# A hybrid attention and delta-rule block: the conditioning projection in four column groups, and four projection units in the prologue

## The chip, the cores and the metric

The kernel runs on one core of a Trainium2 chip. The metric is the time of one execution on the device in microseconds (us): 898.84, the median of 3 runs (898.61 to 899.08).

## What is computed

x is 512 rows of 1024. A vector c of 1024 gives shift and scale (and a gate, used at the end) by a product with w_ada; the normalised x is scaled and shifted and becomes h. h is projected by w_in onto many blocks of columns, which feed a sparse attention branch and a gated delta-rule branch. Both are merged by gates, projected by w_o and added to x.

```python
mod = c @ w_ada + b_ada                      # (1, 3072)
shift, scale, gate = jnp.split(mod, 3, axis=-1)
h = rmsnorm(x, pre_norm_gain) * (1.0 + scale[:, None, :]) + shift[:, None, :]
proj = h @ w_in                              # (512, 10840)
# attention branch: partial_rope on q, k and on the indexer's q_idx, k_idx
# (angles = positions * inv_freq), indexer scores, top 128 keys, softmax
# delta branch: conv of width 4 and silu on q, k, v; per chunk a triangular
# inverse, then a scan over the chunks
y = jax.nn.sigmoid(ga) * y_a + jax.nn.sigmoid(gb) * y_b
return x + gate[:, None, :] * rmsnorm(y @ w_o, post_norm_gain)
```

## The kernel before

All data are float32. Work is kept transposed: 128 channels on the partitions, 512 positions along the free dimension. One projection of h onto 128 columns is a **unit**. Weights are split into a high part (fp32r, made by ScalarE, L926) and a low part (made by GpSimd, L1216), h likewise, and a unit is 8 k tiles times 3 matmuls of 512 columns (L588 to L590), accumulated in one PSUM bank. The list UNITS (L57) gives the order: S (a small unit with the indexer's key and the decay columns), the keys K0 to K5, the indexer's queries I0 to I3, gates GA0 to GA3, then for each head Q, V, Z and one more, then the attention's units, and the merge. The weights of a unit go through a ring of four buffers, its result through three PSUM banks; the unit that takes a bank waits until the one three before it has been read (take_wait, L417).

The order of the work is written out by hand in **rounds**: each round r has a quarter of a unit on TensorE (two k tiles, six matmuls, `part`, L600), and every engine's program has a loop over r in which each step stands in a round of its own. R_KEY, R_LOW, R_GRAM, R_INV, R_DELTA, R_ATT and others (L79 to L87) say in which round the steps of a head begin: the taps of the key's convolution on VectorE (L1552), the decay tiles, the Gram matrix and its norms, the inversion of 16x16 blocks for four heads at a time (`invert`, L1599, 30 dependent small steps, then through DRAM into the tiles U and T), the solve and scan of the delta rule. In a round TensorE does the scan, solve, attention, Gram, small and logit matmuls first and its quarter unit last (L870 to L884).

Ahead of the rounds is the prologue. SyncE issues all loads in one queue: the small rows, constants, x (2 MB), positions, two small vectors, eight tiles of w_ada (1 MB each, whole rows), then weights. VectorE makes four rotary tables' arguments for two frequency sets side by side, 128x1024 (L1364 to L1391); ScalarE takes their sines (L937 to L939). TensorE computes c @ w_ada as matmuls with c broadcast to 128 columns (the tile cb) as the stationary operand and 512 columns of w_ada moving, in four banks (`condition`, L625): 32 fp32 matmuls, 64 instructions, half ahead of the transposes of x and half behind. Each row of the result is the same vector, so VectorE takes the diagonal of sixteen 128x128 blocks by a multiply with the identity and a reduction (L1404) to have it on the partitions. Then h is made per k tile: scale and shift on VectorE (L1416), high part on ScalarE (L948), low part on VectorE (L1420), and TensorE does the units S and K0 k by k behind it (L646 to L650). Round 0 starts with unit 2 (K1).

Of the kernel before, what the change touches and what calls it, by code (L numbers as in the profile page):

```python
# [15 lines left out]
P = 128  # L16
# [29 lines left out]
(C_ID, C_TRIU, C_TRIL, C_FILL, C_ONES, C_M16, C_M32, C_MLOW, C_MUP) = range(9)  # L46
N_CST = 9
SUB = 16

# [7 lines left out]
UNITS = ([("S", 0), ("K", 0)] + [("K", h) for h in range(1, 6)] + [("I", n) for n in range(4)]  # L57
# [10 lines left out]
N_ROUNDS = 4 * (Q_OUT - 2)  # L68


def begins(kind, h):
    return 4 * (UNITS.index((kind, h)) - 2)
# [12 lines left out]
R_ATT = [192] + [188 + 16 * h for h in range(1, HEADS)]  # L85
# [6 lines left out]
def constants():  # L92
# [50 lines left out]
def program(nc, ctx, x, c, positions, w_ada, b_ada, pre_gain, post_gain, w_in, ln_gain, ln_bias, conv_w, a_log,  # L143
# [19 lines left out]
    cols = place("cols", [P, 4 + SUB * SUB])  # L163
# [108 lines left out]
    def bank(b):  # L272
        return ps[:, b, :]
# [48 lines left out]
    def steps(name, names):  # L322
        return Steps(sem(name), names)

    s_rows, s_cst, s_pos, s_x, s_sc, s_bc, s_xres, s_out = (sem(n) for n in (
        "rows_loaded", "constants_loaded", "positions_loaded", "x_loaded", "scalars_loaded", "gate_rows_loaded",
        "residual_loaded", "output_stored"))
    s_ada = [sem(f"w_ada_loaded{k}") for k in range(KT)]
# [11 lines left out]
    pro_pe = steps("pro_pe", ["rowsT", "rows2T"] + [f"x{k}" for k in range(KT)] + ["mod"])  # L340
    pro_act = steps("pro_act", [f"ssq{i}" for i in range(NT)] + ["sinA", "sinI", "cos"] + [f"x{k}" for k in range(1, KT, 2)]
                    + [f"hi{k}" for k in range(KT)])
    pro_dve = steps("pro_dve", ["pcol", "pcol2", "cb", "hgain", "posf", "angA", "angI", "turns", "whole", "r1", "r2", "r3", "rc",
                                "wrap", "rc2", "clamp", "clampc"]
                    + [f"xn{i}" for i in range(NT)] + [f"x{k}" for k in range(0, KT, 2)]
                    + [f"m{b}" for b in range(16)] + ["mb", "scg", "h0"]
                    + [f"{a}{k - (a == 'lo')}" for k in range(1, KT) for a in ("h", "lo")] + [f"lo{KT - 1}"])
# [73 lines left out]

    def unit_bank(kind, h):
        return UNITS.index((kind, h)) % PROJ_BANKS
# [8 lines left out]
    def _(sp):  # L432
        sp.dma_start(prow[R_CONV:R_CONV + 96, :], conv_w.rearrange("w (m p) -> (w m) p", p=P)).then_inc(s_rows, 16)
# [3 lines left out]
        for r, v in ((R2_LNG, ln_gain), (R2_LNB, ln_bias)):  # L437
            for n in range(2):
                sp.dma_start(prow2[r:r + 1, n * IDX_DIM:(n + 1) * IDX_DIM],
                             v.rearrange("(a n) -> a n", a=1)).then_inc(s_rows, 16)  # L440
        sp.dma_start(prow2[R2_NG:R2_NG + 1, :], norm_gain.rearrange("(a n) -> a n", a=1)).then_inc(s_rows, 16)
        sp.dma_start(cst[:], cst_in).then_inc(s_cst, 16)
        sp.dma_start(cols[:], cols_in).then_inc(s_cst, 16)
        sp.dma_start(x_sb[:], x.rearrange("(i p) d -> p i d", p=P)).then_inc(s_x, 16)
        sp.dma_start(pos_i[:], positions.to_broadcast([P, S])).then_inc(s_pos, 16)
        sp.dma_start(small_cols[:, 48:56], a_log.rearrange("(a n) -> a n", a=1).to_broadcast([P, 8])).then_inc(s_sc, 16)
        sp.dma_start(small_cols[:, 56:64], dt_bias.rearrange("(a n) -> a n", a=1).to_broadcast([P, 8])).then_inc(s_sc, 16)
        for k in range(KT):
            sp.dma_start(w_ada_sb[:, k, :], w_ada[k * P:(k + 1) * P, 0:2 * D]).then_inc(s_ada[k], 16)
# [5 lines left out]
        wv = w_in.rearrange("(k p) n -> p k n", p=P)  # L455
        n_ik = IDX_DIM + IDX_HEADS
        sp.dma_start(raw[:, 0, :, 0:n_ik], wv[:, :, COL_IK:COL_IK + n_ik]).then_inc(s_raw[0], 16)
        sp.dma_start(raw[:, 0, :, n_ik:N_SMALL], wv[:, :, COL_BETA:COL_BETA + 2 * HEADS]).then_inc(s_raw[0], 16)
# [80 lines left out]
        for q in range(1, RING):  # L539
            load(q)  # L540
        for r in range(-13, N_ROUNDS + 8):
            if (r - 3) % 4 == 0 and RING <= (r - 3) // 4 + 8 < len(UNITS):
                load((r - 3) // 4 + 8)
# [35 lines left out]
    def _(pe):  # L579

        def project(q, rhs_hi, rhs_lo, ks, m=P):

            slot, out_ap = q % RING, ps[0:m, q % PROJ_BANKS, :]
# [16 lines left out]
        def part(r):  # L600

            q, quarter = r // 4 + 2, r % 4
            kind = UNITS[q][0]
            if quarter == 0 and q >= PROJ_BANKS:
                take_wait(pe, q - PROJ_BANKS)
# [13 lines left out]
        EARLY = 4  # L619
        pe.wait_ge(s_rows, 16 * 9)  # L620
        pe.wait_ge(s_cst, 32)
        pe.transpose(ps[:, 2, 0:P], prow[:], ident).then_inc(*pro_pe.inc("rowsT"))
        pe.transpose(ps[:, 2, P:P + 3], prow2[:], ident[0:3, 0:3]).then_inc(*pro_pe.inc("rows2T"))

        def condition(ks):  # L625
            for k in ks:
                pe.wait_ge(s_ada[k], 16)
                for n in range(4):
                    mm = pe.matmul(bank(2 + n), cb[:, k, :], w_ada_sb[:, k, n * S:(n + 1) * S], start=(k == 0),  # L629
                                   stop=(k == KT - 1))  # L630
            return mm

        pe.wait_ge(*pro_dve.at("cb"))
        pe.wait_ge(*pro_dve.at("pcol2"))
        condition(range(EARLY))
        XB = [0, 1, 6, 7]
        for k in range(KT):
            if k == 0:
                pe.wait_ge(*pro_dve.at(f"xn{NT - 1}"))
            if k >= 4:  # L640
                pe.wait_ge(*(pro_dve if k % 2 == 0 else pro_act).at(f"x{k - 4}"))
            for i in range(NT):
                mm = pe.transpose(ps[:, XB[k % 4], blk(i)], x_sb[:, i, blk(k)], ident)
            mm.then_inc(*pro_pe.inc(f"x{k}"))
        condition(range(EARLY, KT)).then_inc(*pro_pe.inc("mod"))
        for k in range(KT):  # L646
# [26 lines left out]
        def logits(r):  # L673

            for m, (hd, qt) in enumerate(LOGITS):
                if r != ends_at("I", hd // 2) + 4 + m % 6 // 2:
                    continue
# [1165 lines left out]
```

## Time and profile before

| | |
|---|---|
| median of 3 runs | 898.84 us |
| profiled execution | 899.64 us |
| its span | 897.8 us |
| mean granted TensorE clock | 0.983 of full |
| ScalarE busy | 326.7 us, 36% |
| GpSimd busy | 392.6 us, 44% |

The span runs from the first to the last instruction that the profiler recorded on the core; some 1.8 us of the profiled execution lie around it. Busy time is the time in which an engine has at least one instruction running. Matmuls overlap each other, so a matmul's own duration is longer than the distance from its start to that of the next, and a busy TensorE is not a TensorE at its peak. TensorE's granted clock is given as a share of full speed.

### The profile page before, as it was taken

The page shows a single profiled execution, that of the slowest core. Times are in us where ns is not written, and L with a number is a line of the kernel's source. Part 1 is how long each engine was busy: PE and PEld are TensorE (multiplying, and loading weights), DVE is VectorE, ACT ScalarE, POOL GpSimd, SP SyncE. Part 2 cuts the span into 40 slices and gives each one's busy share as a digit, 9 for nine tenths or more (in the row PEclk, how much of TensorE's full clock was granted, in tenths as well). Part 3 has the DMA queues.
Part 4 walks back from the last instruction along what each step waited for, and adds up shares of the span by engine and source line. Part 5 has one row for each costly group of instructions (what it writes and reads, how often), then busy time and mean ns, then how long its engine had stood idle before and what let it go on. Part 6 is the DMA issues. An engine that isn't in the chain of part 4 may idle for free.

```text
span 897.8 us, 11319 instructions
## 1 busy us (share of the span) xinstructions
PE 832.9 (93%) x4226; PEld 672.3 (75%) x4226; DVE 473.0 (53%) x907; ACT 326.7 (36%) x678; POOL 392.6 (44%) x262
## 2 busy tenths in 40 slices
PE   1978688999999989999999999999999999999996
PEld 0546565688888778888888777777777788878996
DVE  3455889826668777665666544445434433232104
ACT  2424432444352434425434344443334322212211
POOL 1123554355264434644535544354543543543542
PEclk9989889999999999999999999999999999999998
DMA  7933530533232332323221222232222245452502
GB/s 273 334 88 124 171 92 8 120 103 110 63 104 61 106 81 61 93 61 106 83 70 48 71 70 71 71 92 72 71 71 71 74 142 160 141 171 86 194 19 94
DMA packets 147345, 92.10 MB, mean 103 GB/s; under 512 B 17746, under 2 KB 140883, under 8 KB 146011
## 3 DMA queue, kind: packets, MB, share of 16 engines
q1 hardware_dynamic: 147290, 91.38, 34.9%
q8 instruction: 34, 0.56, 0.3%
q14 instruction: 21, 0.16, 0.1%
HBM read 84.52 MB, written 6.85 MB: 102 GB/s over the span
## 4 chain that ended last, share of the span: by engine, by line
PE 71%; DVE 18%; ACT 4%; issue 3%; DMA 2%; POOL 1%; SPq 0%; POOLq 0%; ACTq 0%; DVEq 0%
PE ps L588 15%; PE ps L590 15%; PE ps L589 15%; PE ps L629 3%; DVE yq L1552 2%; PE ps L859 2%; PE ps L907 2%; PE ps L906 2%; PE ps L905 2%; PE ps L846 2%; DVE binv L1611 2%; ACT prob L1144 2%; DVE kraw L1552 1%; DMA pos_i<-in_positions 1%; DVE prob L1721 1%
## 5 line engine op out<-in xcount | busy, mean ns | idle before, releaser
L1216 POOL TENSOR_TENSOR w_lo<-raw,w_hi 128x1024 fp32r<-128x1024 f32 (+1 forms) x109 | 263.5, 2423 | 351.5 <-ACT w_hi L926 351.4
L588 PE MATMUL ps<-h_hi,w_hi 128*128 128x512 f32 (+1 forms) x680 | 291.0, 428 | 6.0 <-ACT h_hi L948 6.0
L590 PE MATMUL ps<-h_hi,w_lo 128*128 128x512 f32 (+1 forms) x680 | 269.1, 396 | 0.0
L589 PE MATMUL ps<-h_lo,w_hi 128*128 128x512 f32 (+1 forms) x680 | 267.7, 394 | 0.0
L588 PEld LDWEIGHTS ps<-h_hi,w_hi 128*128 128x128 f32 (+1 forms) x680 | 129.8, 191 | 32.5 <-ACT h_hi L948 6.8
L590 PEld LDWEIGHTS ps<-h_hi,w_lo 128*128 128x128 f32 (+1 forms) x680 | 128.8, 189 | 29.8 <-issue 0.5
L589 PEld LDWEIGHTS ps<-h_lo,w_hi 128*128 128x128 f32 (+1 forms) x680 | 129.7, 191 | 26.1 <-issue 3.6
L926 ACT ACTIVATE w_hi<-raw 128x1024 fp32r<-128x1024 f32 (+1 forms) x109 | 113.3, 1050 | 18.2 <-PE ps L907 17.1
L1085 ACT ACTIVATE o_tok<-ps 128x128 f32<-128x128 f32 x32 | 8.9, 278 | 107.4 <-PE ps L811 107.2
L629 PE MATMUL ps<-w_ada_sb,cb 128*128 128x512 f32 x64 | 30.2, 633 | 11.5 <-DVE rp L1376 11.5
L906 PE MATMUL ps<-w_lo,y_hi 128*128 128x256 f32 x128 | 36.2, 283 | 0.0
L907 PE MATMUL ps<-w_hi,y_lo 128*128 128x256 f32 x128 | 36.2, 283 | 0.0
L905 PE MATMUL ps<-w_hi,y_hi 128*128 128x256 f32 x128 | 36.2, 283 | 0.0
L1726 DVE SCALAR_TENSOR_TENSOR oat<-ps,za 128x512 f32<-128x512 f32 x8 | 5.5, 692 | 55.7 <-PE ps L859 55.7
L629 PEld LDWEIGHTS ps<-w_ada_sb,cb 128*128 128x128 f32 x64 | 12.9, 205 | 27.3 <-issue 15.7
L1738 DVE SCALAR_TENSOR_TENSOR ysum<-th_b,ps 128x512 f32<-128x512 f32 x8 | 5.5, 686 | 51.4 <-PE ps L590 51.4
L1694 DVE TENSOR_TENSOR qk<-qk,sw 32x1024 f32<-32x1024 f32 x8 | 24.6, 3074 | 13.8 <-POOL qk L1313 13.8
L1172 ACT ACTIVATE y_hi<-ysum 128x512 fp32r<-128x512 f32 x8 | 5.1, 633 | 73.5 <-DVE ysum L1749 73.5
L1144 ACT ACTIVATE prob<-prob,amx 128x128 f32<-128x128 f32 (+3 forms) x32 | 17.6, 552 | 30.6 <-DVE amx L1714 30.6
L1313 POOL TENSOR_TENSOR qk<-qk,tab_cos 32x1024 f32<-32x1024 f32 x8 | 27.1, 3382 | 1.1 <-DVE sw L1687 1.1
L1545 DVE MAX8 m<-score 128x8 f32<-128x256 f32 (+2 forms) x48 | 26.5, 551 | 0.0
L1547 DVE MATCH_REPLACE8 score<-m,score 128x256 f32<-128x256 f32 (+2 forms) x48 | 26.1, 543 | 0.0
(274 smaller groups left out, 1445.8 us busy)
## 6 DMA issues: line engine op xcount, KB each, us to landing
raw<-in_w_in SPq DMA_DIRECT2D x84, 512.0 KB, 3.8
w_ada_sb<-in_w_ada SPq DMA_DIRECT2D x8, 1024.0 KB, 19.5
raw<-in_w_b_out SPq DMA_DIRECT2D x8, 512.0 KB, 3.8
raw<-in_w_a_out SPq DMA_DIRECT2D x8, 512.0 KB, 4.1
ada<-in_w_ada SPq DMA_DIRECT2D x8, 512.0 KB, 4.8
raw<-in_w_o SPq DMA_DIRECT2D x8, 512.0 KB, 4.0
inverse_tiles<-zero SPq DMA_DIRECT2D x2, 1032.0 KB, 5.0
x_sb<-in_x SPq DMA_DIRECT2D x1, 2048.0 KB, 10.0
```

The source lines that it names most:

```text
L588: pe.matmul(out_ap, w_hi[:, slot, k, 0:m], rhs_hi(k), start=(k == 0), stop=False)
L589: pe.matmul(out_ap, w_hi[:, slot, k, 0:m], rhs_lo(k), start=False, stop=False)
L590: mm = pe.matmul(out_ap, w_lo[:, slot, k, 0:m], rhs_hi(k), start=False, stop=(k == KT - 1))
L629: mm = pe.matmul(bank(2 + n), cb[:, k, :], w_ada_sb[:, k, n * S:(n + 1) * S], start=(k == 0), stop=(k == KT - 1))
L905: pe.matmul(o_ap, y_hi[k][:, blk(t)], w_hi[:, pair, k, :], start=(k == 0), stop=False)
L906: pe.matmul(o_ap, y_hi[k][:, blk(t)], w_lo[:, pair, k, :], start=False, stop=False)
L907: mm = pe.matmul(o_ap, y_lo[k][:, blk(t)], w_hi[:, pair, k, :], start=False, stop=(k == KT - 1))
L926: act.activation(w_hi[:, slot, :, 0:n], raw[:, slot, :, 0:n], ACT.Copy).then_inc(hi_made, 1)
L1144: act.activation(prob[:, keys(qt)], prob[:, keys(qt)], ACT.Exp, bias=amx[:, 1, qt:qt + 1], scale=HD ** -0.5, accum_out=amx[:, 2, qt:qt + 1 ...
L1216: pool.tensor_tensor(w_lo[:, slot, :, 0:n], raw[:, slot, :, 0:n], w_hi[:, slot, :, 0:n].bitcast(F32), ALU.subtract).then_inc(lo_made, 1)
L1313: pool.tensor_tensor(qk2[h % 2][0:32, :, :], qk2[h % 2][0:32, :, :], tab_cos[0:32, 0:1, :].to_broadcast([32, 2, S]), ALU.mult).then_inc(*r ...
L1552: dve.scalar_tensor_tensor(out=y[:, n:S], in0=src[:, 0:S - n], scalar=pcol_at(R_CONV + (3 - n) * 24 + j * 8, h), in1=y[:, n:S], op0=ALU.mu ...
```

## The change

- **w_ada in four column groups.** Group g holds 256 columns of the shift and the same 256 of the scale, all eight k tiles: two loads of 1 MB in rows of 1 KB. VectorE multiplies the k tiles 0 to 5 by c (one per partition) and adds them up (`mod_sum`); TensorE reduces over the partitions with 12 fp32 matmuls that have one moving column: for each of four 128-column blocks the k tiles 6 and 7 against c, and `mod_sum` against ones. The result is on the partitions at once; the sixteen diagonal reductions and the tile cb go. Three small VectorE ops per group then give shift and scaled gain.
- **h per group.** ScalarE makes h (Identity with scale and bias) and its high part for two k tiles per group, and VectorE the low part. All copies of the transposed x are on ScalarE, four banks in turn.
- **Four units in the prologue.** S, K0, K1 and K2 accumulate k by k as h arrives, in four banks (S in bank 7): S and K0 with k 0 to 3, then K1 and K2 with k 0 to 3, then all four with k 4 to 7. Round 0 starts with unit 4 (K3), and there are eight rounds fewer.
- **Rotary tables.** Both frequency sets share one 128x512 argument: partitions 32 to 63 carry the main one. Four sines; the main tables are made on partitions 32 to 63 of `tab_a` and moved to partitions 0 to 31 by two loads.
- **Queues.** x goes in four tiles on ScalarE's queue, with the small rows behind it; positions and the first constants lead SyncE's queue.
- **Rounds.** In TensorE's loop `part(r)` stands first. The key, decay, Gram, inversion and logit steps have new rounds; where the new number is the old one less eight, nothing moves against the units.

```diff
-UNITS = ([("S", 0), ("K", 0)] + [("K", h) for h in range(1, 6)] + [("I", n) for n in range(4)]
+FIRST_UNITS = 4
+UNITS = ([("S", 0)] + [("K", h) for h in range(6)] + [("I", n) for n in range(4)]
...
-N_ROUNDS = 4 * (Q_OUT - 2)
+N_ROUNDS = 4 * (Q_OUT - FIRST_UNITS)
...
-R_KEY = [ends_at("K", h) for h in range(HEADS)]
-R_LOW = [10, 11, 13, 14, 17, 18, 46, 50]
-R_GRAM = [13, 15, 17, 19, 22, 26, 74, 90]
-R_INV = [25, 97]
+R_KEY = [0, 2, 4, 6, 9, 12, ends_at("K", 6), ends_at("K", 7)]
+R_LOW = [8, 9, 10, 11, 13, 14, 38, 42]
+R_GRAM = [10, 13, 16, 19, 22, 25, ends_at("K", 6) + 5, ends_at("K", 7) + 5]
+R_INV = [27, R_GRAM[7] + 6]
+R_LOGIT = [ends_at("I", m // 6) + 6 + m // 6 + m % 6 // 2 for m in range(24)]
...
+        conditioning(0)
+        load_small()
+        load(1)
+        conditioning(1)
+        load(2)
+        load(3)
+        conditioning(2)
+        conditioning(3)
+        sp.dma_start(cst[:, 2:, :], cst_in[:, 2:, :]).then_inc(s_cst, 16)
+        sp.wait_ge(*pro_act.at("cosA"))
+        sp.dma_start(tab_sin[0:32, 0, :], tab_a[32:64, 0, :]).then_inc(s_tab, 16)
+        sp.dma_start(tab_cos[0:32, 0, :], tab_a[32:64, 1, :]).then_inc(s_tab, 16)
...
+        def conditioning(g):
+
+            pe.wait_ge(s_ada[g], 32)
+            pe.wait_ge(*pro_dve.at(f"a{g}_{DIRECT[0] - 1}"))
+            if g < 2:
+                pe.wait_ge(*pro_act.at(f"x{KT - 4 + g}"))
+            else:
+                pe.wait_ge(*pro_dve.at(f"g{g - 2}"))
+            for n in range(2):
+                for t in range(2):
+                    out_ap = ps[:, 3 + g % 2, 2 * n + t:2 * n + t + 1]
+                    for k in DIRECT:
+                        pe.matmul(out_ap, w_ada_sb[:, g, n, k, blk(t)], pcol[:, 0, R_C + k:R_C + k + 1], start=(k == DIRECT[0]),
+                                  stop=False)
+                    mm = pe.matmul(out_ap, mod_sum[:, g, n, blk(t)], ones[:, 0:1], start=False, stop=True)
+            mm.then_inc(*pro_pe.inc(f"mod{g}"))
...
+        conditioning(0)
+        conditioning(1)
+        first_rows((0, 1), (0, 1))
+        conditioning(2)
+        first_rows((0, 1), (2, 3))
+        first_rows((2, 3), (0, 1, 2, 3))
+        conditioning(3)
+        first_rows((0, 1, 2, 3), (4, 5, 6, 7))
...
         for r in range(N_ROUNDS):
+            part(r)
             for h in range(HEADS):
                 scan(h, r - R_DELTA[h])
...
-            part(r)
...
+        def conditioned(g):
+
+            act.wait_ge(*pro_dve.at(f"g{g}"))
+            for k in (2 * g, 2 * g + 1):
+                act.wait_ge(*pro_act.at(f"x{k}"))
+                act.activation(xT[:, k, :], xT[:, k, :], ACT.Identity, scale=small_cols[:, 24 + k:25 + k],
+                               bias=small_cols[:, 8 + k:9 + k]).then_inc(*pro_act.inc(f"h{k}"))
+                act.wait_ge(*pro_act.at(f"h{k}"))
+                act.activation(h_hi[:, k, :], xT[:, k, :], ACT.Copy).then_inc(*pro_act.inc(f"hi{k}"))
...
+        for g in range(GROUPS):
+            conditioning(g)
+            if g > 0:
+                low_rows(2 * g - 2)
+                low_rows(2 * g - 1)
+            modulation(g)
+        low_rows(KT - 2)
+        low_rows(KT - 1)
```

## Rows read from the trace of the kernel before

**Rows 1.** The page, part 1: busy us, share of the span, instructions.
```profile
PE 832.9 (93%) x4226; PEld 672.3 (75%) x4226; DVE 473.0 (53%) x907; ACT 326.7 (36%) x678; POOL 392.6 (44%) x262
```

**Rows 2.** Stretches, all engines: length, busy us (instructions), granted clock, DMA share, GB/s.
```profile
0.00:60.00 60.00, 34.49 (x99) 17.16 (x100) 22.64 (x64) 16.73 (x23) 11.55 (x12) 0.99 0.76 260
60.00:62.00 2.00, 2.00 (x6) 1.40 (x5) 2.00 (x5) 1.26 (x2) 0.00 (x0) 0.50 0.00 0
73.40:185.90 112.50, 93.24 (x388) 71.05 (x387) 96.57 (x184) 46.16 (x90) 53.70 (x41) 0.92 0.37 96
185.90:195.50 9.60, 9.60 (x44) 7.96 (x43) 0.03 (x1) 3.30 (x7) 4.66 (x3) 1.00 0.54 146
195.50:897.80 702.30, 682.22 (x3654) 566.63 (x3652) 347.11 (x648) 256.36 (x553) 319.85 (x204) 1.00 0.31 90
```

**Rows 3.** Timeline of the prologue: start, duration, engine, line, operation [idle before, releaser].
```profile
14.69 1.06 ACT L932 ACTIVATE xT<-x_sb 128x1024 f32<-128x1024 f32 x1 [12.69 <-DMA x_sb<-in_x]
20.27 2.00 POOL L1228 TENSOR_TENSOR small_cols<-small_cols,nhalf 128x4 f32<-128x4 f32 x1
26.49 2.73 DVE L1395 TENSOR_SCALAR x_sb<-x_sb,small_cols 128x1024 f32<-128x1024 f32 x4
36.27 3.66 PE L643 MATMUL ps<-cst,x_sb 128*128 128x128 f32 x32
53.70 0.29 DVE L1404 CUSTOM_DVE_ANT_0 scratch<-ps,cst 128x128 f32<-128x128 f32 x1 [13.48 <-PE ps L629]
59.65 0.70 PE L588 MATMUL ps<-h_hi,w_hi 128*88 128x512 f32 x1 [5.98 <-ACT h_hi L948]
```

**Rows 4.** Timeline, TensorE: cold matmuls, two Gram groups, last matmuls of units 13 and 14.
```profile
61.43 0.63 PE L589 MATMUL ps<-h_lo,w_hi 128*128 128x512 f32 x1
61.85 0.63 PE L590 MATMUL ps<-h_hi,w_lo 128*128 128x512 f32 x1
...
97.86 1.05 PE L698 MATMUL ps<-kraw 128*128 128x128 f32 x8
...
109.53 2.05 PE L698 MATMUL ps<-kraw 128*128 128x128 f32 x8 [7.88 <-DVE L L1595]
...
189.95 0.39 PE L590 MATMUL ps<-h_hi,w_lo 128*128 128x512 f32 x1
...
195.39 0.39 PE L590 MATMUL ps<-h_hi,w_lo 128*128 128x512 f32 x1
```

**Rows 5.** Timeline of VectorE and GpSimd: first tap, one swish twice, last score fill.
```profile
74.42 2.32 DVE L1552 SCALAR_TENSOR_TENSOR kraw<-ps,pcol,kraw 128x511 f32<-128x511 f32 x3 [7.72 <-ACT kraw L999]
...
100.73 2.77 POOL L1216 TENSOR_TENSOR w_lo<-raw,w_hi 128x1024 fp32r<-128x1024 f32 x1 [0.70 <-ACT w_hi L926]
...
101.33 2.73 DVE L1557 SCALAR_TENSOR_TENSOR kraw<-tz,kraw 128x512 f32<-128x512 f32 x1
...
109.30 0.68 DVE L1557 SCALAR_TENSOR_TENSOR kraw<-tz,kraw 128x512 f32<-128x512 f32 x1
...
185.71 0.22 DVE L1531 TENSOR_SCALAR score<-cst 128x128 f32<-128x128 f32 x1
```

**Rows 6.** DMA: GB/s in 40 slices of 0:40 and 35:55; one issue, KB, landing.
```profile
GB/s 0 33 33 1 51 249 369 223 283 336 299 414 406 360 147 274 328 426 434 426 426 418 434 434 418 434 418 442 410 418 434 434 410 410 375 289 140 66 183 348
GB/s 318 260 188 91 75 57 143 222 349 347 336 290 289 293 289 292 251 91 86 219 333 331 72 136 263 348 287 66 183 322 347 154 96 243 340 321 49 0 0 0
x_sb<-in_x SPq DMA_DIRECT2D x1, 2048.0 KB, 10.0
```

**Rows 7.** Waits of VectorE (73 to 196 us), then of TensorE (195 on): us, times, longest.
```profile
DVE kraw L1552 <- ACT kraw L999: 9.7, 2, 7.7
DVE score L1521 <- ACT relu L988: 4.4, 6, 1.7
...
PE ps L795 <- DVE resid L1664: 6.5, 8, 1.6
...
PE ps L739 <- DVE Zs L1625: 0.2, 1, 0.2
```

More of the change, by code:

```diff
@@ L338, in program @@
     hi_made, lo_made, unit_done = sem("hi_made"), sem("lo_made"), sem("unit_done")
[L340 to L347, printed above, removed]
+    pro_pe = steps("pro_pe", ["rowsT", "rows2T"] + [f"x{k}" for k in range(KT)] + [f"mod{g}" for g in range(GROUPS)])
+    pro_act = steps("pro_act", [f"ssq{i}" for i in range(NT)] + ["sinI", "cosI", "sinA", "cosA"] + [f"x{k}" for k in range(KT)]
+                    + [f"{a}{k}" for k in range(KT) for a in ("h", "hi")])
+    pro_dve = steps("pro_dve", ["posf", "ang", "turns", "whole", "r1", "r2", "r3", "rc", "wrap", "rc2", "clamp", "clampc",
+                                "pcol", "pcol2", "hgain", "ba1"] + [f"xn{i}" for i in range(NT)]
+                    + [step for g in range(GROUPS) for step in
+                       [f"a{g}_{k}" for k in range(KT) if k not in DIRECT]
+                       + [f"lo{k}" for k in range(2 * g - 2, 2 * g) if g > 0]
+                       + [f"m{g}", f"s{g}", f"g{g}"]] + [f"lo{KT - 2}", f"lo{KT - 1}"])
     pro_pool = steps("pro_pool", ["half", "eps_k", "ms", "rstd", "kpadE", "kpadO", "zero"])
@@ L537, in gate_rows @@
             sp.dma_start(ada[1][:], post_gain.rearrange("(a n) -> a n", a=1).to_broadcast([P, D])).then_inc(s_bc, 16)
[L539 to L543, printed above, removed]
+        conditioning(0)
[10 more added lines that the diff above has]
+        sp.dma_start(tab_cos[0:32, 0, :], tab_a[32:64, 1, :]).then_inc(s_tab, 16)
+        for r in range(-21, N_ROUNDS + 8):
+            if (r - 3) % 4 == 0 and RING <= (r - 3) // 4 + 6 + FIRST_UNITS < len(UNITS):
+                load((r - 3) // 4 + 6 + FIRST_UNITS)
             if r == 0:
@@ L600, in part @@
         def part(r):
-            q, quarter = r // 4 + 2, r % 4
+            q, quarter = r // 4 + FIRST_UNITS, r % 4
             kind = UNITS[q][0]
-            if quarter == 0 and q >= PROJ_BANKS:
+            if quarter == 0:
                 take_wait(pe, q - PROJ_BANKS)
@@ L617, in part @@
                 project(q, h_rhs, hl_rhs, ks)
-        EARLY = 4
+        pe.wait_ge(s_first, 32)
         pe.wait_ge(s_rows, 16 * 9)
[L621 to L636, printed above, removed]
+        pe.transpose(ps[:, 7, 0:P], prow[:], ident).then_inc(*pro_pe.inc("rowsT"))
+        pe.transpose(ps[:, 7, P:P + 3], prow2[:], ident[0:3, 0:3]).then_inc(*pro_pe.inc("rows2T"))
         for k in range(KT):
@@ L945, in _ @@
+        split(0, N_SMALL)
+        split(1)
+        conditioned(0)
+        split(2)
+        split(3)
+        for g in range(1, GROUPS):
+            conditioned(g)
+        for q in range(FIRST_UNITS, FIRST_UNITS + 2):
             split(q)
-        for k in range(KT):
-            act.wait_ge(*pro_dve.at(f"h{k}"))
-            act.activation(h_hi[:, k, :], xT[:, k, :], ACT.Copy).then_inc(*pro_act.inc(f"hi{k}"))
         def small(r):
@@ L1195, in _ @@
                 mix(n, r)
-            if r % 4 == 1 and RING <= r // 4 + 4 < len(UNITS):
-                split(r // 4 + 4)
+            if r % 4 == 1 and RING <= r // 4 + 2 + FIRST_UNITS < len(UNITS):
+                split(r // 4 + 2 + FIRST_UNITS)
         mix(KT - 1, N_ROUNDS)
@@ L1242, in _ @@
         pool.memset(zero[:], 0.0).then_inc(*pro_pool.inc("zero"))
+        for q in range(FIRST_UNITS, FIRST_UNITS + 2):
+            split(q)
         def small(r):
@@ L1332, in _ @@
                     index_rows(n)
-            if r % 4 == 1 and RING <= r // 4 + 4 < len(UNITS):
-                split(r // 4 + 4)
+            if r % 4 == 1 and RING <= r // 4 + 2 + FIRST_UNITS < len(UNITS):
+                split(r // 4 + 2 + FIRST_UNITS)
         for q in range(Q_OUT + 2, Q_OUT + 8):
```

231 lines of the change are left out of this document (123 added, 108 removed).

## The prediction

> **What bounds the kernel now.** I read the busy shares first: TensorE is busy for 93% of the span, VectorE for 53% [rows 1]. Then the table by stretch [rows 2]. From 195.5 us on TensorE is busy 682.2 of 702.3 us at full clock, so whatever lets it reach that point sooner comes off the end. Before it there are two stretches with another limit. Up to 60 us TensorE is busy for only 34.5, and those are the conditioning matmuls, not projections. From 73.4 to 185.9 us VectorE is busy for 96.6 of 112.5 and TensorE for 93.2 at a mean clock of 0.92: VectorE sets the pace. From 185.9 to 195.5 VectorE does nothing and TensorE finishes the gate projections. So the prediction is the time at which unit 15 (Q of head 0) can start, 195.6 us now (the last matmul before it starts at 195.39 [rows 4]), and a small term for what follows.
>
> **Prologue, as it is.** x (issued behind the constants) lands at 14.7, ScalarE squares it in four pieces of 1.06 and a short accumulator read each, to about 19.4, GpSimd's two steps end at 22.3, but the normalisation waits until 26.5 because VectorE works on the rotary tables, and it ends at 29.2. TensorE runs 32 conditioning matmuls, the 32 transposes (3.66) and 32 more to 53.7; VectorE's sixteen reductions begin at 53.70, the first projection at 59.65 [rows 3]. Its first matmuls start 0.42 to 0.43 apart at a granted clock of 0.50 (the 1.2 GHz level, after six idle us); at 2.4 GHz the 24 matmuls of a unit take 5.44, 0.227 each (195.39 less 189.95) [rows 2, 4]. S and K0 are complete at 73.3, and VectorE's first tap starts at 74.42 [rows 5].
>
> **Prologue, changed.** x is issued first on ScalarE's queue, at about 0.7. With the 10.0 us from issue to landing of now [rows 6] it lands at 10.7; with no gain at all, at 14.7. I take 12, as half of its company is the same bytes. The table chain is half as wide and starts with positions that are first in their queue; it ends before 12 and no longer delays anything. So: last square 13.3, GpSimd's two steps 2.9 more, 16.2; normalisation 2.7 [rows 3], 19.0. Transposes: 3.66 at full clock, twice that cold; the nearest pair of rows is the Gram group, eight instructions in 1.05 and in 2.05 [rows 4]. TensorE has been idle, so I take 7.3: 26.5. ScalarE's eight copies of about 0.6 fit beside them.
> Then four groups in series:
> - VectorE's sum over six k tiles: one 128x512 multiply (0.44) and five multiply-adds (0.65 each, the price of the 128x512 swish, 0.68, less its overlap [rows 5]), 3.8 us, 15 in all four groups.
> - TensorE's step: 12 fp32 matmuls, 24 instructions, at eight in about 0.92 us (1.05 with the tail [rows 4]): 2.7; cold 5.4. I take 3.5 for the first two, 2.8 for the others.
> - VectorE's three small ops, 0.2 each: 0.6.
> Group 0: its sum is ready early; 26.5 + 3.5 + 0.6 = 30.6. Group 1: sum 3.8 and 3.0 for GpSimd's low splits that now run beside it, 37.4; TensorE 40.9; 41.5. First rows of S and K0 (12 matmuls, cold, 0.427): 46.0. Group 2: its sum ends at 47.3 with 2.0 for the same neighbour; TensorE 50.1. Then 12 + 24 matmuls at 0.227: 8.2, to 58.3. Group 3: its sum is long done, 2.8 and 0.6: 61.7; the last 48 matmuls overlap the small ops' wait and take 10.9: 72.0. Shaving the allowances where ScalarE's and TensorE's steps overlap, I take 71 for S, K0, K1 and K2 complete. Ends: 64 (warm throughout, no collision, x at 10.7) and 80 (cold throughout, every split in the way).
> w_ada's arrival is hidden: 8 MB in 1 KB rows, even at the 290 GB/s that loads in 512-byte rows hold for some us now, against 434 GB/s for its long rows [rows 6], gives about 12.4 MB / 0.29 = 43 us for everything, and group 3's sum starts near 50. Without that cover each us late would count in full. In SyncE's queue the later weight loads now stand behind a wait for the last cosine, near 18; the first of them waits for a split to be done near 29 anyway, so that wait is free.
>
> **The collision.** A VectorE op that takes 0.68 alone took 2.73 while GpSimd's split (2.77, from 100.73) ran, and ended 0.56 after it [rows 5]. Such lengthening is in the 3.0 and 2.0 above; four splits at most 2.4 each, 8.6, would be the upper end, and 0 the lower.
> The Trainium skill ("SBUF — State Buffer", "SBUF: two separate sides") calls the port pair of VectorE and GpSimd an exclusive lock held for the whole instruction: this row agrees. By that rule alone all 24 sums are exposed, and it speaks against moving the reduction to VectorE; with every split in the way the sum would be the 8.6 less the 5.0 taken, 3.6 us later.
>
> **The VectorE stretch.** From its first tap to the last score fill (74.4 to 185.9 [rows 2, 5]) VectorE has 96.6 us of work, and none of it goes away: taps, Gram steps, inversion, logits. What changes is the order. The inversion moves from round 17 (in the new count, eight less than now) to 27, Gram from 5-18 to 10-25, the last logits from 34 to 39. Of the 15.9 idle us of now [rows 2] 2.0 are a wait for a key not yet projected (the other 7.7 of the 9.7 shown lie before 74.4), 4.4 for relu [rows 7], the rest smaller waits for Gram and gaps. With K0 to K2 ready at once and TensorE's part placed first, I take 9 idle. Bounds: 3, and 16 as now.
> So the last fill is at 71 + 1.1 + 97 + 9 = 178. It stands in round 40 and Q begins in 44: four rounds of six matmuls at 0.227, 5.4 us, 183.5. Now there are eight rounds between, 185.9 to 195.6. The inverse goes to DRAM and back in this time: finished some 7 us before the last fill, it needs about 8 (store, two loads), ready near 179, before TensorE wants it in round 45. If VectorE is late there, this is the next wait.
> Gain at Q: 195.6 - 183.5 = 12.
>
> **After it.** Placing the quarter unit before the scan and solve steps gives VectorE one quarter (six matmuls, 1.36) more between a unit's end and the small step that follows. TensorE's waits after 195 are 6.5 us on the residual (eight times, up to 1.6) and seven smaller kinds down to 0.2 [rows 7], 10.7 in all. They come when VectorE's taps are late for the step behind them. I take 6 of gain; bounds 0 and 11, and -3 if the later position delays the scan instead. The later rounds of K6, K7, rope and attention are the old ones less eight, so nothing. The extra queue traffic (two 32-row table moves, the second constants) and the smaller tables cost nothing on the path.
>
> **Sum.** 899.6 (this execution; the span is 897.8 and 1.8 lie around it) - 12 - 6 = 881.6; the median of the runs is 0.8 lower, so **881 us**.
>
> **Rivals.**
> - *VectorE packs tight* (chance 0.22). The stretch has no stall to speak of and the prologue is warm: 64 + 1.1 + 97 + 3 + 5.4 = 170.5, a gain of 25 there, 6 to 9 behind: about 866. For it: VectorE was already 86% busy [rows 2]. Against: the chains through ScalarE in the logits.
> - *The prologue eats the gain* (0.17). TensorE stays at the 1.2 GHz level between its short steps, and the splits block the sums: 80 us instead of 71, idle 13: 196.5 at Q, nothing gained there; 6 less behind: about 893. For it: six idle us were enough for a cold start at 59.65 [rows 3, 4].
> - *Slower* (0.05): the quarter unit ahead. If each small step of the scan now finds its input a quarter later and VectorE's answer does not fit before the next quarter, each of some 30 such steps in a head loses up to 0.2 us over eight heads, 48 at most; from 18 us on it outweighs the rest: 900 to 910.
> - *The groups do not stream*: the sums wait for w_ada after all (1 KB rows far below the 290 GB/s). Group 3 at 60 instead of 43 costs 6: 887; inside my case.
>
> **Numbers.** Forecast 0.56, own range 873 to 889; the rivals as above. The range that takes in the costs' bounds is 863 to 893. Faster by over 0.2% (1.8 us, what a measurement of this kernel can tell from no change): 0.93; within: 0.03; slower: 0.04.
>
> **What would show it.** First projection near 41 us, four units complete near 71; VectorE over 90% busy from there to about 178; unit 15 starting near 183; residual waits after it well under 6.5. Wrong if the four units complete after 80, if VectorE idles over 16 us in its stretch, or if TensorE's time from unit 15 to the end is not 702 us or less.

## The result, and the profile after

The changed kernel takes **904.18 us** (median of 5 runs) where the kernel before, timed beside it, takes 899.08 (the median of five runs, the three behind the 898.84 among them): a ratio of 1.0056, with a 95% interval of 1.0045 to 1.0068. It is slower by some 5 us; 881 was forecast. The profiled execution took 904.26 us, with a span of 902.5; that of before took 899.6, with 897.8.

Part 1 of the page after, beside [rows 1]:

```profile
PE 824.3 (91%) x4258; PEld 680.1 (75%) x4258; DVE 474.7 (53%) x896; ACT 333.3 (37%) x691; POOL 391.0 (43%) x262
```

TensorE has 9 us less work and the span is 5 us longer. The table by stretch says where, beside [rows 2] (columns as there: length, busy us of TensorE, its weight loads, VectorE, ScalarE and GpSimd with the number of instructions, granted clock, DMA share, GB/s; the stretches are from the first tap to the last score fill, from there to the start of unit 15, from there to the end):

```profile
77.80:188.40 110.60, 90.57 (x375) 69.41 (x376) 92.48 (x184) 45.56 (x92) 54.45 (x43) 0.92 0.36 103
188.40:189.50 1.10, 1.10 (x6) 0.93 (x5) 0.02 (x1) 0.00 (x0) 0.00 (x0) 1.00 1.04 296
189.50:902.50 713.00, 685.63 (x3653) 569.79 (x3652) 344.68 (x648) 255.32 (x553) 320.52 (x204) 0.99 0.32 91
```

[rows 2] begins its stretch at 73.4, a microsecond ahead of the first tap at 74.4. Unit 15 starts at 189.5 instead of 195.5, so 6 us are gained up to there. From there to the end it takes 713.0 us instead of 702.3, and 10.7 are lost. Two of the waits in this last stretch are new beside [rows 7] (us, times, longest):

```profile
PE ps L752 <- DMA U<-inverse_tiles: 5.9, 1, 5.9
PE ps L839 <- DVE vnew L1724: 5.7, 3, 2.0
PE ps L830 <- DVE resid L1738: 4.8, 6, 1.8
```

**The first new wait** is for the inverse of the first four heads to come back from DRAM. Its last VectorE copy, then SyncE's queue, then TensorE (timeline: start, duration, engine, line, operation):

```profile
179.09 0.39 DVE L1691 COPY binv<-binv 128x256 f32<-128x256 f32 x1
...
179.15 0.32 SPq L515 DMA_DIRECT2D binv<-lower_tiles  x1
179.51 0.49 SPq L484 DMA_DIRECT2D raw<-in_w_in  x1
180.05 0.58 SPq L505 DMA_DIRECT2D lower_tiles<-L  x1
184.59 0.32 SPq L515 DMA_DIRECT2D binv<-lower_tiles  x1
184.95 1.11 SPq L484 DMA_DIRECT2D raw<-in_w_in  x2
186.17 5.43 SPq L526 DMA_DIRECT2D inverse_tiles<-binv  x2
191.64 0.96 SPq L484 DMA_DIRECT2D raw<-in_w_in  x1
192.64 0.62 SPq L497 DMA_DIRECT2D P_b<-gc_rows  x1
194.88 0.36 SPq L532 DMA_DIRECT2D U<-inverse_tiles  x1
...
198.79 1.43 PE L752 MATMUL ps<-U,L 128*128 128x128 f32 x5 [5.88 <-DMA U<-inverse_tiles]
```

and the stretch behind it, from the table:

```profile
199.00:204.00 5.00, 5.00 (x16) 4.30 (x17) 1.51 (x4) 1.33 (x3) 4.67 (x3) 0.50 0.08 17
```

VectorE is done at 179.5, and the store (L526) leaves only at 186.17. SyncE works its list in order. The load of head 4's blocks (L515) waits for the inversion's last row step, to 179.15; then L of head 5 is stored (L505), and the load of that head's blocks waits for this very store to land, to 184.59. The two stores of the inverse take 5.43 us of SyncE's time, U's load follows at 194.88, and TensorE goes on at 198.79, 19 us after VectorE's end. The 5.88 us cost twice: up to 204.1 the granted clock is 0.50, the 1.2 GHz level, which takes another 2.7 (half of the 5.3 from 198.8 on, an estimate). In the kernel before the same list stood ahead of the same store, but VectorE's copy ended at 165.2, and TensorE wanted U at 197.5:

```profile
162.60 2.58 DVE L1617 COPY binv<-binv 128x256 f32<-128x256 f32 x1
...
168.34 3.45 SPq L515 DMA_DIRECT2D inverse_tiles<-binv  x2
...
197.45 1.05 PE L717 MATMUL ps<-U,L 128*128 128x128 f32 x8
```

### The profile page after: what moved, and what is told of

It reads as the page before. It is cut to its first block, busy times and chain, and to the rows that moved or that the text cites. A ratio compares the mean times of both kernels' runs of the same rounds, so it can differ in the third digit from the quotient of the medians.

```text
span 902.5 us, 11405 instructions
## 1 busy us (share of the span) xinstructions
PE 824.3 (91%) x4258; PEld 680.1 (75%) x4258; DVE 474.7 (53%) x896; ACT 333.3 (37%) x691; POOL 391.0 (43%) x262
## 4 chain that ended last, share of the span: by engine, by line
PE 68%; DVE 15%; ACT 5%; DMA 4%; issue 3%; SPq 2%; POOL 2%; POOLq 0%; ACTq 0%; DVEq 0%
PE ps L609 16%; PE ps L611 16%; PE ps L610 15%; PE ps L894 2%; DVE yq L1626 2%; PE ps L942 2%; PE ps L941 2%; PE ps L940 2%; PE ps L881 2%; ACT prob L1203 2%; DVE kraw L1626 2%; DVE binv L1685 1%; DVE score L1595 1%; DMA w_ada_sb<-in_w_ada 1%; DVE prob L1795 1%
## 5 line engine op out<-in xcount | busy, mean ns | idle before, releaser
L1626 DVE SCALAR_TENSOR_TENSOR kraw<-ps,pcol,kraw 128x511 f32<-128x511 f32 (+2 forms) x24 | 18.0, 748 | 17.1 <-ACT kraw L1058 16.6
L1619 DVE MAX8 m<-score 128x8 f32<-128x256 f32 (+2 forms) x48 | 26.5, 551 | 0.0
L1884 DVE SCALAR_TENSOR_TENSOR out_sb<-ps,small_cols,gate 128x1024 f32<-128x1024 f32 x4 | 5.1, 1283 | 38.7 <-POOL small_cols L1401 38.7
```

The source lines that it names most:

```text
L1619: dve.max(m8[:, t, :], w).then_inc(*top_dve.inc(f"max{t}{n}"))
L1626: dve.scalar_tensor_tensor(out=y[:, n:S], in0=src[:, 0:S - n], scalar=pcol_at(R_CONV + (3 - n) * 24 + j * 8, h), in1=y[:, n:S], op0=ALU.mu ...
```

## The experiments

Every kernel of this section was timed beside the kernel before, whose median was 899.2 to 899.8 us each time, on three chips in all; a ratio is to that median. A difference between two kernels is that of their ratios times 899.5. One profiled execution can't give it: the first tap starts at 77.8 in the changed kernel and at 75.8 and 77.1 in experiments 1 and 4, whose edits touch nothing ahead of it. The traces say where a difference lies, the ratios how large it is.

**1. The store of the inverse first.**

```
-                if r == R_GRAM[h] + 4:
+                if r == (R_INV[0] + 7 + h if h in (4, 5) else R_GRAM[h] + 4):
                     lower_blocks(h)
```

> The changed kernel, with the last two head pairs' row loads moved on SyncE's list from rounds 31 and 33 to rounds 38 and 39, behind the store of the first inverse (round 36). Theory (the inverse's round trip through SyncE's queue is what opens the query stage late): the store of the first inverse leaves some 4 us or more earlier, TensorE's wait for U's inverse (5.9 us at 193 to 199) goes, and with it most of the 6.8 us at the half clock behind it; the time falls by 7 to 9 us, to 895 to 897. Rival (the load is late by its own transfers, not by SyncE's order): the wait stays within 1.5 us of 5.9, and the time stays within 2 us of 904.

The two loads are those of heads 4 and 5 (L515), and stand in rounds 26 and 29 in the changed kernel, not in 31 and 33 as the text above has it; they move to rounds 38 and 39.

Measured: 896.78, ratio 0.9961 (0.9946 to 0.9976), 8.5 us faster than the changed kernel. Its eight executions range from 893.36 to 898.70, and the profiled one, 893.61, is at the low end. SyncE's queue, and from the table the stretch from unit 15 on:

```profile
177.56 1.33 SPq L526 DMA_DIRECT2D inverse_tiles<-binv  x2
...
182.33 0.36 SPq L532 DMA_DIRECT2D U<-inverse_tiles  x1
```

```profile
187.60:891.80 704.20, 682.77 (x3653) 567.74 (x3651) 344.61 (x648) 255.23 (x553) 319.49 (x203) 0.99 0.32 90
```

The two stores take 1.33 us instead of 5.43 and leave as soon as VectorE's copy has ended, at 177.5. U's load leaves 4.8 us behind that copy instead of 15.4, TensorE's wait is gone, and the stretch takes 704.2 instead of 713.0. The theory holds: of the 10.7 lost behind unit 15's start, 8.8 were SyncE's order in this execution, and the 8.5 by the ratios agrees.

**2. GpSimd's splits held back from the column sums.**

```
-        for q in range(1, RING):
+        split(1)
+        pool.wait_ge(*pro_dve.at("lo1"))
+        for q in range(2, RING):
             split(q)
```

> The changed kernel, with GpSimd's third and fourth of the low splits held back until VectorE has made the second low row, so that no split of GpSimd runs beside group 1's column sums. Theory (the 4.8 us that group 1's sums take beyond those of groups 0, 2 and 3 are the shared port's): group 1's five sums fall from 9.2 to 4 to 5 us, the first projection starts some 4 us earlier than 43.8, and the four units are complete near 72 instead of 76.5; the time falls by 3 to 4 us, to about 900. Rival (the first units wait for their w_ada group or for the low weights instead): the sums get shorter, and the four units end within 1 us of 76.5, time within 1 us of 904.

Measured: 900.75, ratio 1.0014 (1.0005 to 1.0024), 3.8 us faster. The sums of column group 1 and GpSimd beside them, in the changed kernel:

```profile
29.30 1.25 DVE L1463 TENSOR_SCALAR mod_sum<-w_ada_sb,pcol 128x512 f32<-128x512 f32 x1 [1.32 <-DMA w_ada_sb<-in_w_ada]
30.59 7.96 DVE L1466 SCALAR_TENSOR_TENSOR mod_sum<-w_ada_sb,pcol,mod_sum 128x512 f32<-128x512 f32 x5
...
44.79 3.90 DVE L1466 SCALAR_TENSOR_TENSOR mod_sum<-w_ada_sb,pcol,mod_sum 128x512 f32<-128x512 f32 x5
...
32.12 5.09 POOL L1275 TENSOR_TENSOR w_lo<-raw,w_hi 128x1024 fp32r<-128x1024 f32 x2 [1.86 <-ACT w_hi L960]
```

and in this experiment:

```profile
29.82 3.90 DVE L1468 SCALAR_TENSOR_TENSOR mod_sum<-w_ada_sb,pcol,mod_sum 128x512 f32<-128x512 f32 x5
...
35.01 4.67 POOL L1275 TENSOR_TENSOR w_lo<-raw,w_hi 128x1024 fp32r<-128x1024 f32 x2 [5.50 <-DVE h_lo L1474]
```

Five multiply-adds take 3.90 us alone and 7.96 beside two splits of 5.09. The Trainium skill ("SBUF — State Buffer", "SBUF: two separate sides") describes the port pair of the two engines as locked for a whole instruction. The trace agrees in kind: 4.06 us more beside 5.09 us of splits.

**3. The quarter unit last, in the changed kernel; first, in the kernel before.** In both, part(r) changes its place in TensorE's round and nothing else.

> The changed kernel, with the round's quarter unit put back to the end of TensorE's round, as in the kernel before. Theory (the quarter in front costs the first rounds and gives nothing behind): the index key's transposes stand ahead of the first quarter, VectorE's stretch begins 2.6 us earlier, and nothing is lost in the query stage: 899 to 902. Rival (what was predicted of the quarter in front, that it hides 6 us of the waits of the query stage): those waits come back, and the time is 908 to 910.

> The kernel before, with the round's quarter unit in front of TensorE's other steps: this part of the change alone. Theory (from the changed kernel with the quarter put back, which was 1.4 to 2 us faster): it costs 0 to 2 us here as well, 899 to 901. Rival (the prediction's step): it hides 6 us of the query stage's waits, 893.

Measured: the changed kernel with it last, 902.82, ratio 1.0037 (1.0025 to 1.0049), 1.7 us faster. The kernel before with it first, 893.29, ratio **0.9934** (0.9921 to 0.9948), 5.9 us faster. Of the first I had expected the sign, and 2 to 5 us; of the second the opposite. In the changed kernel with the quarter last, VectorE's wait for the index key's transposes (2.6 us) is gone and its stretch takes 108.1 us instead of 110.6; the stretch from unit 15 on takes 713.2, for 713.0. The kernel before with it first, by stretch (first tap to last fill, to unit 15, to the end):

```profile
72.60:183.60 111.00, 96.34 (x402) 73.56 (x401) 98.12 (x184) 45.66 (x88) 56.99 (x43) 0.92 0.37 96
183.60:188.70 5.10, 5.10 (x24) 4.22 (x23) 0.06 (x1) 2.71 (x6) 0.74 (x1) 1.00 0.96 253
188.70:890.50 701.80, 682.02 (x3654) 566.63 (x3652) 348.60 (x648) 255.35 (x553) 318.97 (x204) 1.00 0.32 90
```

From the first tap to unit 15 it takes 116.1 us instead of 121.1, and behind that 701.8 instead of 702.3. So the rival for this run named the right size (893) and the wrong place. In the kernel before, VectorE's last fill ends 9.6 us before unit 15 can start [rows 2]: TensorE is the later engine there. With the quarter in front it projects while VectorE's answer is awaited, and this gap shrinks to 5.1. In the changed kernel it is 1.1 us. VectorE is the later engine, and a TensorE that runs ahead gains nothing.

**4. The Gram steps of heads 6 and 7 a round later.**

```
-R_GRAM = [..., ends_at("K", 6) + 5, ends_at("K", 7) + 5]
-R_INV = [27, R_GRAM[7] + 6]
+R_GRAM = [..., ends_at("K", 6) + 6, ends_at("K", 7) + 6]
+R_INV = [27, R_GRAM[7] + 7]
```

> The changed kernel, with the Gram steps of heads 6 and 7 one round later (66 and 82, which is six rounds behind the end of their key, as in the kernel before; the change has them five behind) and the second inversion at 89 instead of 87. Theory: at round 65 and 81 VectorE does the residual, the Gram step's 3.8 us and then the copy that TensorE waits for, which is why two waits of 2.0 us for vnew stand at 247 and 287 and none did before; one round later the Gram step stands behind the copy, and the third wait (1.7, beside the second inversion) changes too. The waits for vnew fall from 5.7 us to under 2, the time falls by 3 to 4 us, to about 900.5. Rival: the Gram step's 3.8 us only push the next step instead, and the time stays within 1 us of 904.

Measured: 902.13, ratio 1.0030 (1.0019 to 1.0042), 2.3 us faster. VectorE around the second new wait, in the changed kernel:

```profile
245.67 0.68 DVE L1699 TENSOR_TENSOR Zs<-ps,cst 128x512 f32<-128x512 f32 x1
246.26 0.68 DVE L1657 TENSOR_TENSOR diag<-ps,cst 128x512 f32<-128x512 f32 x1
...
248.33 1.13 DVE L1669 SCALAR_TENSOR_TENSOR L<-ps,kst,L 128x128 f32<-128x128 f32 x4
249.38 0.28 DVE L1724 COPY vnew<-ps 128x128 f32<-128x128 f32 x1
```

The Gram step (L1657 to L1669, 3.2 us) stands ahead of the small copy (L1724) that TensorE waits for. One round later the copy comes first, and the 5.7 us of waits for vnew become 1.0; those for the residual and the state rise from 5.3 to 8.2. The waits for vnew fell as expected, all waits together by less, and the time by somewhat less too.

**5. The conditioning wholly on TensorE.** DIRECT is range(8): 32 one-column matmuls a group instead of 12, and no sums on VectorE.

> The changed kernel with the conditioning sums wholly on TensorE: four column groups still, but 32 matmuls a group instead of 12, and no VectorE sums. Theory (VectorE's sums, lengthened by GpSimd's splits, are what the prologue waits for as much as TensorE): 20 more matmuls of two passes, some 4.3 us a group at 2.4 GHz, 17 us in all, against 8 us of idle TensorE that go and 5 us of cold clock that go with them: the four units are complete at 78 to 81 instead of 76.5, the time is 906 to 909. Rival one: the matmuls cost in full, 17 us, 920. Rival two: without sums and collision the prologue ends earlier than 76, and the time is under 903.

Measured: 924.42, ratio 1.0277 (1.0263 to 1.0291), 19.9 us slower. My theory of 906 to 909 was wrong, and rival one is near. Two rows of TensorE's timeline, and two stretches of the table:

```profile
25.04 24.59 PE L664 MATMUL ps<-pcol,w_ada_sb 128*128 128x1 f32 x128
54.69 10.55 PE L664 MATMUL ps<-pcol,w_ada_sb 128*128 128x1 f32 x64
```

```profile
32.00:40.00 8.00, 8.00 (x39) 8.00 (x39) 1.66 (x5) 3.39 (x5) 0.00 (x0) 0.50 1.10 348
40.00:49.00 9.00, 9.00 (x44) 9.00 (x44) 0.11 (x1) 1.28 (x2) 4.68 (x2) 0.50 1.09 305
```

I had priced a group's 20 more matmuls at 2.4 GHz. All but the first 3 us of the first two groups ran at the 1.2 GHz level, 0.21 us an instruction where 0.11 are taken at 1.00, with TensorE busy throughout. VectorE's sums are thus worth 20 us to the changed kernel.

**6. Edits together.** First those of 1 and 2, then those of 1 to 4. In this second kernel and all that follow from it the quarter stands behind the small matmuls and ahead of the logits, not at the very end of the round as in experiment 3 and the kernel before; what that place is worth against the end wasn't run.

> The changed kernel with both edits, the row loads behind the inverse's store and GpSimd's two splits behind the second low row. Theory (two independent losses, one ahead of the stretch that VectorE bounds, one behind it): the gains add, 10 to 13 us, to 891 to 894. Rival (an earlier stretch meets SyncE's store, or the weights, at the same absolute time): no more than the gain of the larger edit alone, 895 to 897.

> The changed kernel with four edits: the row loads behind the inverse's store, GpSimd's two splits behind the second low row, the quarter unit at the end of TensorE's round, and the Gram steps of heads 6 and 7 one round later. Theory (four independent losses): 893.1 with the first two, less 1.4 to 2 for the quarter, less 3 to 4 for the Gram steps: 887 to 889. Rival (with the quarter last the waits for the residual return, or the Gram step's time only moves): 891 to 893.

Measured: 893.05, ratio 0.9930 (0.9915 to 0.9946); and **886.77**, ratio 0.9861 (0.9847 to 0.9874), 17.5 us faster than the changed kernel. Alone the first two gave 8.5 and 3.8, 12.3, and together 11.3; alone the four gave 16.3. They add, as far as intervals of 1 to 1.4 us on each side can tell. Its stretches:

```profile
73.40:181.50 108.10, 91.03 (x372) 69.51 (x372) 92.67 (x184) 45.57 (x93) 54.56 (x44) 0.92 0.45 122
...
182.50:884.90 702.40, 682.28 (x3654) 566.60 (x3652) 347.19 (x648) 256.29 (x553) 319.63 (x203) 1.00 0.32 90
```

Behind unit 15 the time of before, 702.3, is back.

**7. The quarter in front again**, now in that kernel.

> The four-edit kernel (886.8 us) with one edit taken back: the quarter unit in front of TensorE's round again, as the change has it. The kernel before gained 6.2 us from the quarter in front; its stretch from VectorE's first tap to the start of unit 15's successor fell from 121.0 to 116.0 us, with TensorE 9.7 us behind VectorE's last score fill there. Theory (the quarter in front lets TensorE work on while VectorE is awaited, and so pays only while TensorE is the later of the two; in the changed kernel VectorE's fill ends 1 us before the query unit starts, so nothing is left to gain, and the index key's transposes stand behind a stalled quarter): 1 to 2.5 us slower, 888 to 889. Rival (the changed kernel's other losses had hidden the gain, and they are gone now): 880 to 883.

Measured: 889.80, ratio 0.9900 (0.9886 to 0.9915), 3.5 us slower than with it behind the small matmuls. Waits of VectorE from the first tap on, the row that the other kernel lacks:

```profile
DVE sm L1505 <- PE ps L691: 3.6, 1, 3.6
```

VectorE's stretch is 111.8 us instead of 108.1. So the quarter in front is worth -5.9 us where TensorE is the later engine and +3.5 where VectorE is. The index key's transposes (L691) stand behind a quarter that waits for key 0's bank, and VectorE waits for them.

**8. The decay steps later.** Four low decays move by one or two rounds, off ScalarE's list ahead of key 5's copy.

```
-R_LOW = [8, 9, 10, 11, 13, 14, 38, 42]
+R_LOW = [8, 9, 11, 13, 14, 16, 38, 42]
```

> The four-edit kernel (886.8 us), with the decay steps of four heads one or two rounds later (rounds 8, 9, 11, 13, 14, 16 instead of 8, 9, 10, 11, 13, 14), so that none of them stands on ScalarE's list ahead of key 5's copy, for which VectorE waited 3.05 us at 111. Theory (from the first tap to the query stage VectorE alone sets the time): that wait goes, the last fill comes 2 to 3 us earlier, and so does the query stage: 884 to 885. Rival (TensorE or the inverse's round trip is within a microsecond of the end as well): the fill comes earlier and the query stage does not: 886.5.

Measured: **882.10**, ratio 0.9811 (0.9798 to 0.9825), 4.5 us faster, more than expected. ScalarE and VectorE in the kernel of 6, and then the two stretches of this one:

```profile
109.26 1.28 ACT L1071 ACTIVATE L<-L,gsc 128x128 f32<-128x128 f32 x4 [2.46 <-POOL L L1322]
110.44 0.67 ACT L1058 ACTIVATE kraw<-ps,pcol 128x512 f32<-128x512 f32 x1
...
111.14 2.32 DVE L1628 SCALAR_TENSOR_TENSOR kraw<-ps,pcol,kraw 128x511 f32<-128x511 f32 x3 [3.05 <-ACT kraw L1058]
```

```profile
75.20:178.80 103.60, 89.38 (x372) 68.73 (x373) 91.95 (x184) 45.62 (x92) 54.71 (x44) 0.93 0.48 127
...
179.80:882.10 702.30, 682.25 (x3654) 566.58 (x3652) 348.89 (x648) 256.12 (x553) 318.64 (x203) 1.00 0.32 90
```

VectorE's stretch is 103.6 us instead of 108.1: the 3.05 of waiting are gone, a wait of 0.7 for the Gram matmuls too, and there is 0.7 less work. Unit 15 starts 1.0 behind the last fill as before, and the stretch behind it is the same to 0.1 us. In this pair of executions the first tap came 1.8 later (75.2 for 73.4), so 2.7 arrive at unit 15 and 2.8 at the end; the ratios give 4.5, the whole of the stretch. A wait taken off VectorE's chain comes off the time, so that chain sets it there. By its median it is also the fastest of all kernels run, 17 us under the kernel before, and all that differs from the change is an order: SyncE's, GpSimd's, TensorE's round and three tables of rounds.

**9. TensorE kept at work in the prologue.** First 52 transposes in the idle time ahead of group 1, in the kernel of 6. Then 64, and four more ahead of each output column of groups 1 and 2, in the kernel of 8.

> The four-edit kernel (886.8 us), with 52 transposes of 128x128 that nobody reads, between TensorE's steps for column group 0 and 1, where it stood idle for 7.5 us. Their results are not used. In the four-edit kernel TensorE's granted clock was 0.50 from about 30 to 43 and again from 46.5 to 53. Theory (the idle time costs twice, once itself and once in the clock behind it): the step of group 1 takes 2.6 us instead of 5.1 and the first rows 0.23 instead of 0.43 us a matmul, at least the first of the two cold stretches goes: four units complete 3 to 7 us earlier, 880 to 884. Rival (the group sums on VectorE or w_ada's arrival set the time of each group's step, so a warm TensorE only waits more): within 1.5 us of 886.8.

> The kernel with five edits (882.1 us), with 64 transposes of 128x128 that nobody reads between TensorE's steps for column group 0 and 1, and four such transposes ahead of each of the four output columns of groups 1 and 2. Their results are not used. With 52 of them between the steps alone the clock stayed at 2.4 GHz until group 1's one-column matmuls had run for some 2 us and was at 1.2 GHz from about 36 to 43, and again behind group 2's. Theory (an idle engine followed by one-column matmuls is what loses the clock; wide ones between them keep it): no half-clock stretch before 50, which takes some 2.5 us off group 1's step, 2.4 off the twelve first rows and 4 behind group 2, and adds 16 transposes of 0.11, 1.8 us, in each of the two groups: 3 to 6 us faster, 876 to 879. Rival (the clock falls all the same, for what the other engines and the transfers do at that time): the added transposes cost 3 to 5 us, 885 to 887.

Measured: 886.28, ratio 0.9859 (0.9846 to 0.9873), no difference; and 885.39, ratio 0.9832 (0.9811 to 0.9853), 1.9 us slower than the kernel it comes from, with intervals that overlap. Both are what the rivals had (within 1.5 us of 886.8; 885 to 887). The prologue of the second, by stretch:

```profile
36.00:38.00 2.00, 2.00 (x21) 2.00 (x20) 0.00 (x0) 0.00 (x0) 2.00 (x2) 1.00 1.08 345
38.00:40.00 2.00, 2.00 (x12) 1.63 (x12) 1.40 (x4) 0.00 (x0) 2.00 (x1) 1.00 1.09 345
...
42.00:44.00 2.00, 0.00 (x0) 0.00 (x0) 1.89 (x4) 0.90 (x2) 0.00 (x0) 1.00 1.07 302
...
48.00:50.00 2.00, 2.00 (x11) 2.00 (x11) 0.00 (x0) 0.00 (x0) 0.00 (x0) 0.50 1.06 276
```

The first half-clock stretch is gone and group 1's rows end earlier, but TensorE then idles 3.1 us for group 2's sums on VectorE, and its clock is down from about 46 to 56 after all. With the 16 transposes among them, most at the 1.2 GHz level, group 2's step takes 6.5 us, where it took 4.2 in the kernel of 8. Why the sums don't start earlier, VectorE and GpSimd show, first in the kernel of 6, then in the one with 52 transposes:

```profile
39.75 0.31 DVE L1486 TENSOR_TENSOR small_cols<-small_cols,pcol 128x2 f32<-128x2 f32 x1
39.98 0.47 DVE L1465 TENSOR_SCALAR mod_sum<-w_ada_sb,pcol 128x512 f32<-128x512 f32 x1
35.38 4.66 POOL L1275 TENSOR_TENSOR w_lo<-raw,w_hi 128x1024 fp32r<-128x1024 f32 x2 [5.51 <-DVE h_lo L1474]
```

```profile
38.37 1.88 DVE L1488 TENSOR_TENSOR small_cols<-small_cols,pcol 128x2 f32<-128x2 f32 x1
40.18 0.47 DVE L1467 TENSOR_SCALAR mod_sum<-w_ada_sb,pcol 128x512 f32<-128x512 f32 x1
35.57 4.67 POOL L1277 TENSOR_TENSOR w_lo<-raw,w_hi 128x1024 fp32r<-128x1024 f32 x2 [5.51 <-DVE h_lo L1476]
```

TensorE's step for group 1 ends 1.1 us earlier (38.4 for 39.5), and VectorE's last small op behind it then takes 1.88 us instead of 0.31, to the end of GpSimd's split at 40.2. Group 2's sum starts at 40.0 to 40.2 in these two, and in the kernel of 8 with the added transposes and without. By this reading the splits that experiment 2 had moved there ate TensorE's gain; what a warm TensorE is worth with them out of the way wasn't run.

## Why the prediction was wrong

The sign was wrong. From the profiled execution, step by step:

- **Prologue: 76.5 instead of 71.** Its first half was right: normalisation ends at 18.5 (19.0), the transposes at 24.6 (26.5). Group 1's sum began at 29.3, after 1.3 us of waiting for w_ada, whose arrival was thus not wholly hidden, and took 9.2 us where 6.8 were allowed. Over both groups the collision was sized right, 4.8 us for 5.0, but all of it fell on group 1; group 2's sum took 4.4. More came from TensorE's clock: group 1's step took 5.1 us at the 1.2 GHz level where 3.5 were allowed, group 2's 3.4 where 2.8 were, and the 36 matmuls behind that 10.7 instead of 8.2, the first twelve at that level. "The prologue eats the gain" took its part, not the whole. (Four splits at 2.4 are 9.6, not the 8.6 of the upper end; the forecast doesn't rest on it.)
- **VectorE's stretch: 110.6 instead of 106.** Work 92.5 (97 taken; 184 instructions as in the kernel before, in 4.1 us less), idle 18.1 (9 taken; 16 was my upper bound, and that counts the microsecond ahead of the first tap: 14.9 from there). Against the kernel before the waits for relu and for the Gram matmuls fell, from 7.9 to 1.5, but those for ScalarE's copies rose from 2.0 to 4.8 and for its tanh from 0.6 to 3.0, and the index key's transposes behind the stalled quarter (2.6) are new. Experiment 8 shows that the order of one list of ScalarE was worth 4.5 us.
- **Fill to unit 15: 1.1 instead of 5.4.** With the two steps above and 1.3 us to the first tap (1.1 taken), unit 15 starts at 189.5, not at 183.5: 6.0 us late.
- **"It needs about 8 (store, two loads), ready near 179, before TensorE wants it in round 45": the step that failed.** The round trip took 19 us: 6.7 until the store leaves, 5.4 for its issue, 3.2 to U's load and 3.9 for that to land. I had priced the transfers, and not what stands ahead of them on SyncE's list. In the kernel before this list had cost nothing, for 32 us lay between VectorE's copy and TensorE's use; the change leaves 13.4 (179.5 to 192.9, where the 5.9 us of waiting begin). That is 5.9 of wait and 2.7 of clock; experiment 1 gives back 8.5.
- **"I take 6 of gain" for the quarter in front, behind unit 15: half a microsecond.** With the quarter in front the stretch of 702.3 became 701.8 in the kernel before, and that of 702.4 became 701.9 in the repaired one. The waits for the residual, which I had counted up, are the same 6.5 us with the quarter in front or behind (experiments 6 and 7). The gain of 6 exists in the kernel before, ahead of unit 15. In the change the gap that it came from is down to 1.1 us, I take it because of the two units more; these alone weren't run.
- **"The later rounds of K6, K7 ... are the old ones less eight, so nothing".** The Gram rounds of these two heads are the old ones less nine, and that single round was worth 2.3 us.

In sum: 881.6, 6.0 late at unit 15, and 16.7 behind it (10.7 lost where 6.0 gained were forecast), 904.3 against 904.26. Of the 10.7, 5.9 and 2.7 are the inverse and its clock and 1.4 the other waits; the rest, under a microsecond, stays open. The time lies in the range of the rival *slower* (900 to 910), but not by its mechanism: there the quarter in front was to cost each small step of the scan, and putting it back gives 1.7 us, none of it behind unit 15. Where VectorE was to idle over 16 us, and the time from unit 15 was not to be 702 or less, the prediction had said that it would be wrong: both came true. What it says of w_ada's sums was right in kind; experiment 5 shows that they save 20 us against TensorE alone.

## What to carry to other kernels

Before an edit that brings work forward on one engine, ask which engine is the later one at the point where both meet, and by how much: that slack (9.6 us here) bounds what such edits can gain together, and the quarter in front, worth 5.9 us alone, cost 1.7 to 3.5 on top of the units ahead. When a step is moved in a schedule written out by hand, replay every in-order queue around it, SyncE's too: a load that waits for its own store and stands ahead of an urgent one is harmless until its cover is gone, and then it made a trip of 19 us. And a plan that comes out slower may need only another order: the same work took 904 us and 882.

## What the runs showed of the hardware

- TensorE's granted clock fell while the profile had it 100% busy. In experiment 5 one-column matmuls ran back to back from 25 to 49 us, and from about 28 on the granted clock was 0.50, the 1.2 GHz level. Before it fell TensorE had run 128-column transposes, at 1.00, and then 3 us of the one-column matmuls. With 52 such transposes in the gap (experiment 9) it stood at 1.00 to about 36, and fell 2 us into group 1's one-column matmuls, ahead of which 1.8 us were idle. The Trainium skill ("TensorE: Matmul & The Clock Gate", "What's actually happening") has the level follow how busy the engine has lately been. By the profile's busy time this trace doesn't show that: it read 100% at either level.
- The issue of the same two stores held SyncE's queue for 5.43 us at 186, 3.45 in the kernel before and 1.33 at 177.6 in experiment 1. Weight loads had been issued just ahead of it in the first two, and 4 us or more ahead in the third; whether they set the time wasn't separated.
